# Long convolution on TensorE: 128-row products with four column blocks on shifted copies, in place of diagonal weights

## The chip, the cores and the metric

The kernel runs on one core of a Trainium2 chip. The metric is device time in microseconds of one execution. Five engines run side by side: TensorE (matrix products into PSUM), VectorE (DVE), ScalarE (ACT), GpSimd (POOL) and SyncE (SP), which here only issues transfers. They are ordered by semaphores alone.

## The reference

Two transformer-like blocks over 256 tokens with 1,024 features, all in float32. The part that the change touches is the convolution module at the very start:

```python
def conformer_conv(x, norm_g, pw1_w, pw1_b, dw_w, dw_b, ln_g, ln_b, pw2_w, pw2_b):
    a, b = jnp.split(rmsnorm(x, norm_g) @ pw1_w + pw1_b, 2, axis=-1)
    h = a * jax.nn.sigmoid(b)
    h = lax.conv_general_dilated(h, dw_w[:, None, :], window_strides=(1,),
        padding=[(CONV_WIDTH - 1, 0)], dimension_numbers=('NWC', 'WIO', 'NWC'),
        feature_group_count=h.shape[-1]) + dw_b
    h = jax.nn.silu(layernorm(h, ln_g, ln_b))
    return h @ pw2_w + pw2_b
```

The convolution is depthwise and causal with CONV_WIDTH = 31: each feature has its own 31 taps, output[t] = sum over j of tap[j] times input[t - 30 + j]. After it come two feed-forward layers, an attention with three branches, a gated recurrence, cross attention and a last feed-forward layer.

## The kernel before

Features lie on partitions: 1,024 features are KT = 8 feature tiles of 128, each with S = 256 tokens in the free dimension. `u` [128, 8, 30 + 256] holds the gated input of the convolution behind 30 zero columns, `v` [128, 8, 256] its output, `tapT` the taps, one column per tap.

**Weights and their queue.** Every dense weight comes in chunks of 1 MB, in one fixed order, through four `raw` buffers, all issued by SP (L464 to L472). Chunks 0 to 7 are `pw1` (one per feature tile, two transfers of 512 KB each), 8 to 11 `pw2` (one transfer each), from 12 on the first feed-forward layer. Chunk c waits until DVE has finished splitting chunk c - 4. ACT takes the high part of a chunk (`split_hi`, L568), DVE the low part (`split_lo`, L936), and TensorE forms three products (L1461 to L1463) for each pair of tiles. There are three split slots, so that ACT's split of a chunk also waits for TensorE to have finished the chunk three before. `through(c)` stands in the streams of ACT and DVE wherever the splits up to chunk c are to be done.

**The first stage.** TensorE runs eight `feature_pair("pw1", ft, ...)` of 48 products each. After each, ACT takes a sigmoid (L636, `gate_act`) and DVE multiplies (`glu_pw1`, L986, counted by `glu_done`) into `u`. `glu_pw1(ft)` first does the split of chunk ft + 2.

**The convolution.** Feature tiles 0 to 3 and 28 taps of tile 4 (`SHARED`) are done by DVE, one multiply-add of 128x256 per tap and tile (L1015, L1018), in two passes over the 31 taps: tiles 0 and 1, then 2, 3 and 4. Every fourth tap one entry of `tasks` is put in: the remaining `glu_pw1` and the splits of the `pw2` chunks. Tiles 5 to 7 and the last 3 taps of tile 4 are done by TensorE as products with a diagonal 128x128 matrix per tap (L1593, 96 products), after all eight `pw1`. ACT builds the diagonals (`diagonals`, L626) in the buffer `act`, eight to a group, between its splits, and copies the finished sums out (L661, `conv_out`).

**After it.** TensorE sums `v` over the features with a constant matrix (L1603; in order the tiles 5, 6, 7, 0 to 4), DVE subtracts the mean (L1038), ACT squares, and so on to `pw2`, which waits for all of it. Nothing of the layers behind can start earlier.

Of the kernel before, what the change touches and what calls it, by code (L numbers as in the profile page):

```python
# [33 lines left out]
P = 128  # L34
# [17 lines left out]
TAPG = 8  # L52
# [15 lines left out]
def build_kernel(nc, a, out):  # L68
# [8 lines left out]
    with ctx:  # L77
# [81 lines left out]
        CONV_DVE, SHARED, SHARED_TAPS = 4, 4, 28  # L159
        pe_taps = {ft: list(range(SHARED_TAPS if ft == SHARED else 0, TAPS)) for ft in range(CONV_DVE, KT)}  # L160

        groups = [(ft, js[i:i + TAPG]) for ft, js in pe_taps.items() for i in range(0, len(js), TAPG)]
        NDIAG = 7
        diag = actf[:, 0:NDIAG * TAPG * P].rearrange("p (g t c) -> p g t c", t=TAPG, c=P)

# [41 lines left out]
        conv_link = sem("conv_link")  # L207
        conv_dve = sem("conv_dve")
# [22 lines left out]
        diag_built = sem("diag_built")  # L231
        diag_used = sem("diag_used")
# [227 lines left out]
        def _(sp):  # L460
            for t in range(TT):
                sp.dma_start(h[:, t, :], a["x"][0].rearrange("(t p) n -> p t n", p=P)[:, t, :]
                             ).then_inc(x_loaded[t], 16)
            for c, parts in enumerate(chunks):  # L464
                if c >= RAWS:
                    last = c - RAWS
                    if is_split[last]:
                        sp.wait_ge(*lo_count(last))
                    else:
                        sp.wait_ge(*freed[last])  # L470
                for place, src in parts:
                    sp.dma_start(place(raw[c % RAWS]), src).then_inc(raw_loaded[c % RAWS], 16)  # L472
# [86 lines left out]
        def _(sc):  # L559
# [61 lines left out]
            def diagonals(g):  # L621
                ft, js = groups[g]
                if g >= NDIAG:
                    sc.wait_ge(diag_used, g - NDIAG + 1)
                for q, j in enumerate(js):
                    x = nc.scalar.activation(diag[:, g % NDIAG, q, :], ident[:, :], ACT.Copy,  # L626
                                             scale=tapT[:, ft, j:j + 1])
                x.then_inc(diag_built, 1)


            for ft in range(KT):
# [20 lines left out]

            built = NDIAG
            for ft in range(CONV_DVE, KT):
                used = max(g for g in range(len(groups)) if groups[g][0] == ft) + 1
                while built < min(used + NDIAG, len(groups)):
                    diagonals(built)
                    built += 1
                if ft != SHARED:
                    sc.wait_ge(diag_used, used)  # L660
                    nc.scalar.activation(v[:, ft, :], bank[ft][:, 0:S], ACT.Identity,  # L661
                                         bias=vecT[:, col["a_dw_b"] + ft:col["a_dw_b"] + ft + 1]
                                         ).then_inc(conv_out, 1)
# [261 lines left out]
        def _(ve):  # L925
# [47 lines left out]
            nc.vector.memset(u[:, :, 0:PAD], 0.0).then_inc(pads_zero, 1)  # L973

# [25 lines left out]
            tasks = [lambda ft=ft: glu_pw1(ft) for ft in range(2, KT)]  # L1000
# [3 lines left out]
            for fts in ((0, 1), (2, 3, SHARED)):  # L1004
                for j in range(TAPS):
                    if j % 4 == 3 and tasks:
                        tasks.pop(0)()
                    if SHARED in fts and j == SHARED_TAPS:
                        fts = fts[:-1]
                    for f, ft in enumerate(fts):  # L1010
                        tap, dst, src = tapT[:, ft, j:j + 1], v[:, ft, :], u[:, ft, j:j + S]
                        b = col["a_dw_b"] + ft
                        if j == 0:
                            ve.wait_ge(glu_done, ft + 1)
                            x = nc.vector.tensor_scalar(dst, src, tap, vecT[:, b:b + 1], ALU.mult, ALU.add)  # L1015
                        else:
                            ve.wait_ge(conv_link, tap_done[ft])
                            x = nc.vector.scalar_tensor_tensor(out=dst, in0=src, scalar=tap, in1=dst,  # L1018
                                                               op0=ALU.mult, op1=ALU.add)
                        if j == TAPS - 1:  # L1020
                            x.then_inc(conv_dve, 1)
                        else:
                            taps_done += 1
                            tap_done[ft] = taps_done
                            x.then_inc(conv_link, 1)

            ve.wait_ge(diag_used, 1 + max(g for g in range(len(groups)) if groups[g][0] == SHARED))
            ve.wait_ge(conv_link, tap_done[SHARED])
            nc.vector.tensor_tensor(v[:, SHARED, :], v[:, SHARED, :], bank[SHARED][:, 0:S],
                                    ALU.add).then_inc(conv_dve, 1)  # L1030
# [408 lines left out]
        def _(te):  # L1439
# [135 lines left out]

            for ft in range(KT):
# [378 lines left out]
```

## Time and profile before

| | us |
|---|---|
| median of 3 runs | 1180.0 (1174.27 to 1182.57) |
| the profiled execution, its own time | 1178.26 |
| its span, first to last instruction | 1176.5 |
| TensorE busy in the span | 1108.6 (94%) |
| DVE / ACT / POOL busy | 665.4 / 548.7 / 64.7 |
| mean granted TensorE clock | 0.973 |

The profile is one execution, recorded instruction by instruction. A float32 product is recorded as two instructions (two passes), so the 96 products of L1593 are x192. A name such as `v` or `act` is the tensor's, without its slice. "Idle before" is an engine's idle time ahead of an instruction, with what ended it. Times in rows are from the span's start.

### The profile page before, as it was taken

The page shows a single profiled execution, that of the slowest core. Times are in us where ns is not written, and L with a number is a line of the kernel's source. Part 1 is how long each engine was busy: PE and PEld are TensorE (multiplying, and loading weights), DVE is VectorE, ACT ScalarE, POOL GpSimd, SP SyncE. Part 2 cuts the span into 40 slices and gives each one's busy share as a digit, 9 for nine tenths or more (in the row PEclk, how much of TensorE's full clock was granted, in tenths as well). Part 3 has the DMA queues.
Part 4 walks back from the last instruction along what each step waited for, and adds up shares of the span by engine and source line. Part 5 has one row for each costly group of instructions (what it writes and reads, how often), then busy time and mean ns, then how long its engine had stood idle before and what let it go on. Part 6 is the DMA issues. An engine that isn't in the chain of part 4 may idle for free.

```text
span 1176.5 us, 17460 instructions
## 1 busy us (share of the span) xinstructions
PE 1108.6 (94%) x7303; PEld 989.8 (84%) x7303; DVE 665.4 (57%) x1104; ACT 548.7 (47%) x888; POOL 64.7 (5%) x102
## 2 busy tenths in 40 slices
PE   6997899999999977999999979999999999999997
PEld 6996589999989954789999979899667888999996
DVE  3999555445445489454555556646454454555554
ACT  5871354444443478354433445535344544444442
POOL 3000073000010000000000010000000000000000
PEclk9999899999999899799999999999899999999999
DMA  8740146566673600546666553654215424555640
GB/s 230 226 128 8 57 123 179 181 204 180 187 151 97 227 1 2 170 135 185 192 195 180 179 179 101 206 179 130 86 40 173 138 80 143 180 193 174 206 144 36
DMA packets 188313, 170.76 MB, mean 145 GB/s; under 512 B 15398, under 2 KB 164006, under 8 KB 188234
## 3 DMA queue, kind: packets, MB, share of 16 engines
q1 hardware_dynamic: 187128, 167.20, 46.4%
q10 hardware_dynamic: 1010, 2.43, 0.6%
q8 instruction: 58, 0.95, 0.3%
q14 instruction: 21, 0.17, 0.0%
q0 software_dynamic: 96, 0.02, 0.0%
HBM read 168.58 MB, written 1.05 MB: 144 GB/s over the span
## 4 chain that ended last, share of the span: by engine, by line
PE 79%; DVE 13%; ACT 3%; POOL 1%; issue 1%; POOLq 0%; ACTq 0%; DVEq 0%
PE bank L1461 24%; PE bank L1462 24%; PE bank L1463 24%; DVE v L1018 5%; DVE split_lo L936 2%; PE bank L1476 1%; ACT scaled L586 1%; DVE soft L1155 1%; DVE soft L1136 1%; PE bank L1639 1%; PE bank L1827 1%; POOL msq L501 1%; PE bank L1826 1%; POOL rstd L504 1%; DVE h L968 0%
## 5 line engine op out<-in xcount | busy, mean ns | idle before, releaser
L936 DVE TENSOR_TENSOR split_lo<-raw,split_hi 128x2048 fp32r<-128x2048 f32 (+1 forms) x157 | 356.1, 2270 | 240.4 <-ACT split_hi L568 240.3
L1461 PE MATMUL bank<-xn_hi,split_hi 128*128 128x256 f32 x1440 | 411.2, 286 | 3.2 <-DVE xn_lo L953 3.1
L1462 PE MATMUL bank<-xn_lo,split_hi 128*128 128x256 f32 x1440 | 408.6, 284 | 0.0
L1463 PE MATMUL bank<-xn_hi,split_lo 128*128 128x256 f32 x1440 | 408.5, 284 | 0.0
L568 ACT ACTIVATE split_hi<-raw 128x2048 fp32r<-128x2048 f32 (+1 forms) x157 | 296.4, 1890 | 148.6 <-PE bank L1463 142.2
L1461 PEld LDWEIGHTS bank<-xn_hi,split_hi 128*128 128x128 f32 x1440 | 277.4, 193 | 7.0 <-issue 5.3
L1462 PEld LDWEIGHTS bank<-xn_lo,split_hi 128*128 128x128 f32 x1440 | 277.5, 193 | 1.3
L1463 PEld LDWEIGHTS bank<-xn_hi,split_lo 128*128 128x128 f32 x1440 | 277.4, 193 | 0.0
L1461 PE MATMUL bank<-split_hi,ffa_hi 128*128 128x512 f32 x320 | 124.9, 390 | 0.0
L1462 PE MATMUL bank<-split_lo,ffa_hi 128*128 128x512 f32 x320 | 124.9, 390 | 0.0
L1463 PE MATMUL bank<-split_hi,ffa_lo 128*128 128x512 f32 x320 | 124.5, 389 | 0.0
L1461 PE MATMUL bank<-split_hi,xn_hi 128*128 128x512 f32 (+3 forms) x240 | 92.3, 385 | 5.1 <-DVE xn_lo L936 5.1
L1463 PE MATMUL bank<-split_hi,xn_lo 128*128 128x512 f32 (+3 forms) x240 | 90.5, 377 | 0.0
L1462 PE MATMUL bank<-split_lo,xn_hi 128*128 128x512 f32 (+3 forms) x240 | 90.5, 377 | 0.0
L684 ACT ACTIVATE soft<-bank 128x256 f32<-128x256 f32 x44 | 16.9, 385 | 137.1 <-PE bank L1463 137.1
L1463 PEld LDWEIGHTS bank<-split_hi,ffa_lo 128*128 128x128 f32 x320 | 60.1, 188 | 12.8
L1461 PEld LDWEIGHTS bank<-split_hi,ffa_hi 128*128 128x128 f32 x320 | 60.2, 188 | 11.6
L1462 PEld LDWEIGHTS bank<-split_lo,ffa_hi 128*128 128x128 f32 x320 | 60.2, 188 | 11.1
L1461 PEld LDWEIGHTS bank<-split_hi,xn_hi 128*128 128x128 f32 x240 | 47.6, 198 | 17.4 <-DVE xn_lo L936 5.0
L1018 DVE SCALAR_TENSOR_TENSOR v<-u,tapT,v 128x256 f32<-128x256 f32 x147 | 58.9, 474 | 0.0
L501 POOL TENSOR_SCALAR msq<-ssq 128x1 f32<-128x1 f32 x20 | 10.5, 527 | 811.2 <-ACT scaled L586 811.0
L1463 PEld LDWEIGHTS bank<-split_hi,xn_lo 128*128 128x128 f32 x240 | 47.5, 198 | 8.2
(257 smaller groups left out, 1042.5 us busy)
## 6 DMA issues: line engine op xcount, KB each, us to landing
raw<-in_ffn_w_in SPq DMA_DIRECT2D x88, 512.0 KB, 5.1
raw<-in_w_ff SPq DMA_DIRECT2D x32, 1024.0 KB, 5.2
raw<-in_ffn_w_out SPq DMA_DIRECT2D x22, 1024.0 KB, 4.9
raw<-in_w_in SPq DMA_DIRECT2D x14, 1024.0 KB, 5.2
raw<-in_a_pw_w SPq DMA_DIRECT2D x16, 512.0 KB, 6.9
raw<-in_w_xkv SPq DMA_DIRECT2D x8, 1024.0 KB, 5.3
raw<-in_a_pw_w SPq DMA_DIRECT2D x4, 1024.0 KB, 5.2
raw<-in_b_w_in SPq DMA_DIRECT2D x4, 1024.0 KB, 6.7
```

What stands on the lines that cost most here:

```text
L501: nc.gpsimd.tensor_scalar(msq[:, c:c + 1], ssq[:, c:c + 1], EPS, None, ALU.add).then_inc(ms_ready, 1)
L504: nc.gpsimd.tensor_tensor(rstd[:, c:c + 1], msq[:, c:c + 1], nhalf[:, 0:1], ALU.pow).then_inc(rstd_ready, 1)
L568: nc.scalar.activation(split_slot[m % SPLITS][0][:, 0:n], raw[c % RAWS][:, 0:n], ACT.Copy).then_inc(split_hi, 1)
L586: nc.scalar.activation(scaled[:, t, :], src[:, t, :], ACT.Square, scale=D ** -0.5, accum_out=ssq[:, TT * k + t:TT * k + t + 1]).then_inc(s ...
L684: nc.scalar.activation(softf[:, b], bank[ft % 4][:, 0:S], ACT.Silu).then_inc(gate_act, 1)
L936: return nc.vector.tensor_tensor(dst, src, hi.bitcast(F32), ALU.subtract)
L1018: x = nc.vector.scalar_tensor_tensor(out=dst, in0=src, scalar=tap, in1=dst, op0=ALU.mult, op1=ALU.add)
L1136: x = nc.vector.tensor_tensor_reduce(out=scores_of(i)[:, piece], in0=src, in1=bias, scale=-DH ** -0.5, scalar=3e38, op0=ALU.add, op1=ALU.m ...
L1155: x = nc.vector.tensor_scalar(scores_of(i)[:, piece], scores_of(i)[:, piece], coef[:, i % 2, n:n + 1], None, ALU.mult)
L1461: mm(dst, left[0], right[0], start=start, stop=False)
L1462: mm(dst, left[0], right[1], start=False, stop=False)
L1463: return mm(dst, left[1], right[0], start=False, stop=stop)
```

## The change

Tiles 0 and 1 stay on DVE, in one pass over the taps. Tiles 2 to 7 (`CONV_PE`) all go to TensorE in another form. For each such tile, SP copies `u` into `quad_u`: for each group of 32 channels q and each shift g of 0 to 3, partitions 32g to 32g+31 hold the 32 channels shifted by g columns, 16 transfers of 32 partitions and up to 1,136 bytes a row. With these, one product of 128 rows (4 shifts x 32 channels) and 32 columns covers four taps of 32 channels; eight such rounds cover the 31 taps (the weight of the 32nd is zero), and four blocks of 32 columns, one for each q, stand side by side in the array: 32 products for a tile. DVE builds the weights of a tile in one multiplication with broadcast operands (`quad_weights`, 128x1024), from `quad_taps`, which TensorE rearranges once (`turn_quads`, 16 products of 64 columns) and DVE copies out of PSUM. The buffers have three slots (`RING`).

The products `conv(0)` to `conv(2)` are put behind `pw1` of tiles 4, 5 and 6, `conv(3)` to `conv(5)` after the last `pw1`. On SP the copies for tile ft stand ahead of the load of chunk ft + 5 and wait for `glu_done` of that tile. ACT builds no diagonals any more and copies six tiles out instead of three.

```diff
-        CONV_DVE, SHARED, SHARED_TAPS = 4, 4, 28
+        QUAD, NQ = 32, P // 32
+        ROUNDS, SPAN = 8, S + 28
+        CONV_DVE = [0, 1]
+        CONV_PE = [2, 3, 4, 5, 6, 7]
+        RING = 3
...
+            def shift_copies(n):
+
+                ft, slot = CONV_PE[n], n % RING
+                sp.wait_ge(glu_done, ft + 1)
+                if n == 0:
+                    sp.wait_ge(quad_set, RING)
+                if n >= RING:
+                    sp.wait_ge(quad_done, n - RING + 1)
+                for g in range(NQ):
+                    w = SPAN - (g == NQ - 1)
+                    for q in range(NQ):
+                        sp.dma_start(quad_u[QUAD * g:QUAD * g + QUAD, slot, q, 0:w],
+                                     u[QUAD * q:QUAD * q + QUAD, ft, g:g + w]).then_inc(quad_loaded[slot], 16)
+
+            conv_at = {ft + RAWS + 1: n for n, ft in enumerate(CONV_PE)}
...
+                if c in conv_at:
+                    shift_copies(conv_at[c])
                 for place, src in parts:
                     sp.dma_start(place(raw[c % RAWS]), src).then_inc(raw_loaded[c % RAWS], 16)
...
-                if ft == 0:
-                    sc.wait_ge(pre_copied, 3)
-                if ft < NDIAG:
-                    diagonals(ft)
...
+            for n, ft in enumerate(CONV_PE):
+                sc.wait_ge(quad_done, n + 1)
+                nc.scalar.activation(v[:, ft, :], bank[4 + n % 4][:, 0:S], ACT.Identity,
+                                     bias=vecT[:, col["a_dw_b"] + ft:col["a_dw_b"] + ft + 1]
+                                     ).then_inc(conv_out, 1)
...
+            for g in range(NQ):
+                q = slice(QUAD * g, QUAD * g + QUAD)
+                x = nc.vector.tensor_copy(quad_one[q, :], ident[q, q])
+            link(x)
+            ve.wait_ge(quad_taps_turned, 1)
+            link(nc.vector.tensor_copy(quad_taps[:, :, :, :].rearrange("p a f j -> p (a f j)"),
+                                       bank[7][:, 0:NQ * KT * ROUNDS]))
+            link(nc.vector.memset(quad_taps[P - QUAD:P, :, :, ROUNDS - 1:ROUNDS], 0.0))
+
+            def quad_weights(n):
+
+                if n >= RING:
+                    ve.wait_ge(quad_done, n - RING + 1)
+                shape = [P, NQ, ROUNDS, QUAD]
+                nc.vector.tensor_tensor(quad_w[:, n % RING, :, :, :],
+                                        quad_taps[:, :, CONV_PE[n], :].unsqueeze(3).broadcast_to(shape),
+                                        quad_one[:, :].unsqueeze(1).unsqueeze(1).broadcast_to(shape),
+                                        ALU.mult).then_inc(quad_built, 1)
+
+            tasks = []
+            for ft in range(2, KT):
+                tasks.append(lambda ft=ft: glu_pw1(ft))
+                if ft - 2 < len(CONV_PE):
+                    tasks.append(lambda n=ft - 2: quad_weights(n))
             tasks += [lambda j=j: through(chunk_of["pw2"][j]) for j in range(3)]
...
-            for fts in ((0, 1), (2, 3, SHARED)):
+            for j in range(TAPS):
+                if j % 4 == 1:
+                    for task in tasks[:2]:
+                        task()
+                    tasks = tasks[2:]
+                for ft in CONV_DVE:
...
+            def conv(n):
+
+                slot = n % RING
+                te.wait_ge(quad_built, n + 1)
+                te.wait_ge(quad_loaded[slot], 16 * NQ * NQ * (n // RING + 1))
+                if n >= 4:
+                    te.wait_ge(conv_out, n - 3)
+                for j in range(ROUNDS):
+                    for q in range(NQ):
+                        x = mm(bank[4 + n % 4][QUAD * q:QUAD * q + QUAD, 0:S], quad_w[:, slot, q, j, :],
+                               quad_u[:, slot, q, 4 * j:4 * j + S], start=j == 0, stop=j == ROUNDS - 1)
+                x.then_inc(quad_done, 1)
+
             for ft in range(KT):
...
+                if ft == 1:
+                    turn_quads()
+                if 4 <= ft < KT - 1:
+                    conv(ft - 4)
+            for n in range(3, len(CONV_PE)):
+                conv(n)
...
-                for q, j in enumerate(js):
-                    x = mm(bank[ft][:, 0:S], diag[:, g % NDIAG, q, :], u[:, ft, j:j + S],
-                           start=j == pe_taps[ft][0], stop=j == TAPS - 1)
-                x.then_inc(diag_used, 1)
```

The sum over features (L1603 of before) takes the tiles 2 to 7 first and 0 and 1 last.

## Rows read from the trace of the kernel before

**Rows 1.** The page: busy time by engine, and the chain that ended last

```profile
PE 1108.6 (94%) x7303; PEld 989.8 (84%) x7303; DVE 665.4 (57%) x1104; ACT 548.7 (47%) x888; POOL 64.7 (5%) x102
PE 79%; DVE 13%; ACT 3%; POOL 1%; issue 1%; POOLq 0%; ACTq 0%; DVEq 0%
```

**Rows 2.** The chain that ended last, 30 to 125 us: start, length, what

```profile
33.78 0.74 DVE v L1015 x2
34.51 1.58 DVE v L1018 x4
36.09 2.20 DVE split_lo L936
38.69 3.16 DVE v L1018 x8
...
84.14 26.93 DVE v L1018 x68
111.11 1.92 PE bank L1603 x6
113.05 2.36 DVE v L1038 x2
```

**Rows 3.** Groups by line and shape, 0 to 160 us: busy, mean ns, idle before

```profile
L1018 DVE SCALAR_TENSOR_TENSOR v<-u,tapT,v 128x256 f32<-128x256 f32 x147 | 58.9, 474 | 0.0
L1593 PE MATMUL bank<-u,act 128*128 128x256 f32 x192 | 41.6, 378 | 0.0
L626 ACT ACTIVATE act<-ident,tapT 128x128 f32<-128x128 f32 x96 | 29.3, 389 | 5.1 <-PE bank L1593 2.6 <-DVE posT L997 1.4 <-issue 1.0
L1038 DVE TENSOR_TENSOR v<-v,bank 128x1024 f32<-128x1024 f32 x2 | 2.4, 1217 | 1.3 <-PE bank L1603 1.3
```

**Rows 4.** Timeline of ACT: sigmoids of pw1 tiles 2 and 7, last copy out

```profile
36.37 0.47 ACT L636 ACTIVATE soft<-bank,vecT 128x256 f32<-128x256 f32 x1 [0.90 <-PE bank L1463]
65.17 0.47 ACT L636 ACTIVATE soft<-bank,vecT 128x256 f32<-128x256 f32 x1 [1.14 <-PE bank L1463]
106.64 0.47 ACT L661 ACTIVATE v<-bank,vecT 128x256 f32<-128x256 f32 x1 [12.92 <-PE bank L1593]
```

**Rows 5.** Timeline of TensorE, 66 to 70 us: start, length, merged instructions

```profile
65.62 4.70 PE L1593 MATMUL bank<-u,act 128*128 128x256 f32 x21
```

**Rows 6.** Timeline, attention, 424 to 427 us: products of 64 columns, two destinations in turn

```profile
425.19 0.20 PEld L1711 LDWEIGHTS bank<-pt,v 128*64 128x64 f32 x4 [0.21 <-issue]
425.19 0.65 PE L1711 MATMUL bank<-pt,v 128*64 128x256 f32 x4
425.67 0.39 PE L1713 MATMUL bank<-pt,v 128*64 128x128 f32 x4
425.89 0.60 PE L1711 MATMUL bank<-pt,v 128*64 128x256 f32 x4
426.32 0.39 PE L1713 MATMUL bank<-pt,v 128*64 128x128 f32 x4
```

**Rows 7.** Timeline of SP: start, length until the queue took it, merged issues

```profile
8.05 0.78 SPq L477 DMA_DIRECT2D pt<-in_cmp_pos_k  x2
8.87 0.88 SPq L477 DMA_DIRECT2D pt<-in_cmp_pos_v  x2
61.38 0.99 SPq L472 DMA_DIRECT2D raw<-in_ffn_w_in  x2
379.75 2.22 SPq L472 DMA_DIRECT2D raw<-in_b_w_out  x1
```

**Rows 8.** Timeline of ACT's own queue: a transfer to 64 partitions

```profile
65.82 0.61 ACTq L646 DMA_DIRECT2D phi<-in_phi_v_w  x1
```

**Rows 9.** DMA issues, 0 to 170 us: KB each, median us from issue to landing

```profile
raw<-in_ffn_w_in SPq DMA_DIRECT2D x12, 512.0 KB, 4.8
raw<-in_a_pw_w SPq DMA_DIRECT2D x4, 1024.0 KB, 5.2
pt<-in_a_norm POOLq DMA_DIRECT2D x1, 4.0 KB, 5.9
```

**Rows 10.** Windows: us, busy of PE, PEld, DVE, ACT, POOL, granted clock, DMA share, GB/s

```profile
20.00:30.00 10.00, 10.00 (x86) 9.78 (x86) 5.46 (x5) 7.15 (x8) 0.00 (x0) 1.00 1.13 294
100.00:110.00 10.00, 8.76 (x41) 7.29 (x39) 10.00 (x26) 0.47 (x1) 0.00 (x0) 1.00 0.00 0
110.00:120.00 10.00, 3.38 (x9) 1.86 (x10) 6.63 (x11) 3.61 (x4) 0.00 (x0) 0.61 0.00 1
```

More of the change, by code:

```diff
@@ L51 @@
 SLOT = 2048
-TAPG = 8
 XSCALE = (D // XH) ** -0.5
@@ L156, in build_kernel @@
         pw2_row = qT[0:1, 0:4, :].rearrange("p a b -> p (a b)")
-        CONV_DVE, SHARED, SHARED_TAPS = 4, 4, 28
[L160 to L164, printed above, removed]
+        QUAD, NQ = 32, P // 32
[3 more added lines that the diff above has]
+        RING = 3
+        quad_u = actf[:, 0:RING * NQ * SPAN].rearrange("p (r a x) -> p r a x", a=NQ, x=SPAN)
+        at = RING * NQ * SPAN
+        quad_w = actf[:, at:at + RING * NQ * ROUNDS * QUAD].rearrange("p (r a j c) -> p r a j c", a=NQ, j=ROUNDS, c=QUAD)
+        quad_taps = ptf[:, 512:512 + NQ * KT * ROUNDS].rearrange("p (a f j) -> p a f j", a=NQ, f=KT)
+        quad_one = ptf[:, 768:768 + QUAD]
         window = ptf[:, 0:2 * 32 * 2 * NCMP].rearrange("p (b l g n) -> p b l g n", b=2, l=32, g=GROUPS)
@@ L207, in build_kernel @@
         conv_link = sem("conv_link")
+        quad_set = sem("quad_set")
+        quad_taps_turned = sem("quad_taps_turned")
+        quad_built = sem("quad_built")
+        quad_loaded = [sem(f"quad_loaded{i}") for i in range(RING)]
+        quad_done = sem("quad_done")
         conv_dve = sem("conv_dve")
@@ L230, in build_kernel @@
         glu_done = sem("glu_done")
-        diag_built = sem("diag_built")
-        diag_used = sem("diag_used")
         conv_out = sem("conv_out")
@@ L973, in _ @@
             nc.vector.memset(u[:, :, 0:PAD], 0.0).then_inc(pads_zero, 1)
+            for r in range(RING):
+                nc.vector.memset(quad_u[P - QUAD:P, r, :, SPAN - 1:SPAN], 0.0).then_inc(quad_set, 1)
             ve.wait_ge(pre_turned, 1)
@@ L1003, in _ @@
             taps_done, tap_done = 0, {}
-            for fts in ((0, 1), (2, 3, SHARED)):
[L1005 to L1030, printed above, removed]
+            for j in range(TAPS):
[4 more added lines that the diff above has]
+                for ft in CONV_DVE:
+                    tap, dst, src = tapT[:, ft, j:j + 1], v[:, ft, :], u[:, ft, j:j + S]
+                    b = col["a_dw_b"] + ft
+                    if j == 0:
+                        ve.wait_ge(glu_done, ft + 1)
+                        x = nc.vector.tensor_scalar(dst, src, tap, vecT[:, b:b + 1], ALU.mult, ALU.add)
+                    else:
+                        ve.wait_ge(conv_link, tap_done[ft])
+                        x = nc.vector.scalar_tensor_tensor(out=dst, in0=src, scalar=tap, in1=dst,
+                                                           op0=ALU.mult, op1=ALU.add)
+                    if j == TAPS - 1:
+                        x.then_inc(conv_dve, 1)
+                    else:
+                        taps_done += 1
+                        tap_done[ft] = taps_done
+                        x.then_inc(conv_link, 1)
@@ L1574, in turn_taps, with turn_quads @@
                 x.then_inc(pre_turned, 1)
+            def turn_quads():
+                te.wait_ge(pre_copied, 2)
+                for q in range(NQ):
+                    for g in range(NQ):
+                        x = mm(bank[7][QUAD * g:QUAD * g + QUAD, KT * ROUNDS * q:KT * ROUNDS * q + KT * ROUNDS],
+                               ident[:, QUAD * q:QUAD * q + QUAD], tapT[:, :, g:g + 4 * ROUNDS:4],
+                               start=True, stop=True)
+                x.then_inc(quad_taps_turned, 1)
+            def conv(n):
[5 more added lines that the diff above has]
+                for j in range(ROUNDS):
+                    for q in range(NQ):
+                        x = mm(bank[4 + n % 4][QUAD * q:QUAD * q + QUAD, 0:S], quad_w[:, slot, q, j, :],
+                               quad_u[:, slot, q, 4 * j:4 * j + S], start=j == 0, stop=j == ROUNDS - 1)
+                x.then_inc(quad_done, 1)
             for ft in range(KT):
```

31 lines of the change are left out of this document (4 added, 27 removed).

## The prediction

> **What bounds the kernel now.** I read the page first: TensorE is busy 94% of the span and holds 79% of the chain, DVE holds 13% of it [rows 1]. That is an average over stages. The chain in order of time shows this stage apart: from 33.78 us on it is DVE without a break, taps and splits, its last piece 68 taps in 26.93 us up to 111.11; TensorE then sums the features for 1.92 us and at 113.05 DVE subtracts the mean [rows 2]. So what the change is worth is how much earlier than 113.05 the mean can be subtracted. Behind it stands a chain that the change leaves alone. TensorE is not far behind DVE: its own 96 tap products take 41.6 us [rows 3] after the last `pw1`, whose sigmoid starts at 65.17, and their last copy out starts at 106.64 [rows 4]. Relieving DVE alone would give 4 us; both must become shorter. ACT's diagonals (29.3 us) lie beside them, and nothing waited for them at length [rows 3].
>
> **DVE, part by part.** A tap costs 0.395 us (8 in 3.16), a split 2.20 [rows 2]. It loses 152 - 62 = 90 taps, 35.6 us, and an addition of 0.4. It gains six `quad_weights`. The nearest row, 128x1024 with a broadcast operand, is 1.22 us [rows 3]; bounds 0.6 (if the operands could be read at double rate, which no row shows) and 1.22, I take 1.2: 7.2 us. The set-up (four 32x32 copies, a 128x256 copy out of PSUM, a memset, three waits on itself) I estimate at 1.2, from 0.4 for a 128x256 operation [rows 2]. Without waits DVE would end at 111.1 - 36.0 + 8.4 = 83.5. It does not run free, as `glu_pw1(7)` needs the last `pw1`.
>
> **TensorE.** A full product of 256 columns is two passes of (4.70 - 0.38)/20 = 0.216 us: 0.43 [rows 5, 3]. What four products of 32 columns cost is the question. No row has four; the nearest has two of 64 columns into the two halves of one bank [rows 6]: four passes of 256 columns take 425.89 to 426.32, 0.43 us, where one after another they would take 0.86. So different column blocks do run at once, and past the second pass of the one before. Four passes of 128 columns take 0.22, that is 0.055 per load and product, so issue would not hold a round of eight passes (0.44). Bounds of a round: 0.43 (all four at once) and 1.72 (one after another); I take 0.43, as the row shows full overlap. A tile is 8 x 0.43 = 3.5 us. The rule that speaks against it is in the Trainium skill, "TensorE: Matmul & The Clock Gate", Part 3: packing small matmuls; three column blocks there gained 2.38 times and four row blocks 3.07, not the full count. By 3.07 a tile would be 4.5 us and the end some 3 us later; the trace's two blocks gained 2.0 of 2.
>
> Each change of block form costs about 0.2 us (the load at 425.19 waited 0.21 with no releaser [rows 6]), two at each of the first three `conv`: 3.9 us each. `turn_quads`, four rounds of four products of 64 columns, is 4 x 0.11 plus two changes and its latency: 1.1.
>
> **SP, the new load.** 96 transfers more, each of 32 partitions, issued one by one ahead of weight loads. The nearest rows are the positions (32 partitions each): two in 0.82 us, then two in 0.93 [rows 7]. I take 0.46 in steady state; below lies 0.41, above 0.61 for one to 64 partitions [rows 8]. 16 of them: 7.4 us. A 1 MB chunk costs 1.0 to issue as two transfers [rows 7], about 0.4 as one. A transfer behind two that are not yet through can be held: 2.22 us in one row [rows 7]. The copies of tile 3 stand right behind chunk 7; I put 1.5 there. The source is SBUF, of which no row shows anything. Landing: a 512 KB load lands in 4.8 us, of which 1.8 is its bytes at 294 GB/s [rows 9, 10]; I take the remaining 3.0 for the last copy, with bounds 0.5 (about the issue alone) and 5.9 [rows 9]. The Trainium skill, "DMA: Bandwidth & Descriptors", anatomy of one DMA, puts the fixed cost of a transfer from POOL at about 2.0 us; by that the end would come 1 us earlier.
>
> **The schedule.** Sigmoids of `pw1` stood 5.76 apart, the third at 36.37 [rows 4]. With 1.1 for `turn_quads` they are at 37.5, 43.2 and 49.0 for tiles 2 to 4, then with `conv(0)` to `conv(2)` at 58.7, 68.3 and 78.0 for 5 to 7.
> - DVE: `glu_pw1(2)` ends two operations after 37.5, at 38.4. From there each period is a split, a product, a `quad_weights` and 8 taps, 2.2 + 0.4 + 1.2 + 3.2 = 7.0. It waits for tile 6 and tile 7 and has `glu_pw1(7)` at 78.9; then 1.2 + 3.2 + 3.2, the split of chunk 10 (2.2), four taps (1.6): 90.3.
> - SP: copies 38.4 to 45.8, chunk 7 and the hold to 48.3, copies to 55.7, chunk 8 (0.4), copies 56.1 to 63.5, then 71.3, 79.1 and the last 79.5 to 86.9. A cycle of 7.8 is just above the 7.0 of DVE, so SP falls behind and sets the end by itself; the copies of tile 7 could have started at 78.9.
> - Loads: chunk 7 is issued at 46 rather than at 34, chunk 8 at 56. They land by 53 and 61 and are wanted by DVE at about 57 and 64; chunk 9 is issued at 64, wanted at 73. No wait, with some 3 us in hand.
> - TensorE: `conv(3)` from 78, `conv(4)` to 86, then idle until the copies land at 89.9, `conv(5)` to 93.4. ACT's copy ends at 94.0. The last three tiles are summed as before, in 1.94 (111.11 to 113.05): 95.9.
>
> The gain is 113.05 - 95.9 = 17.1 us, taken from the profiled execution's own 1178.3 (span 1176.5 and 1.8 around it): 1161.2. The median of the runs is 1.7 higher and their spread is 8.3, so I leave **1161**. ACT loses 96 diagonals and gets three copies out: nothing, as it waits either way. The clock stands at full speed up to 110 and falls to a mean of 0.61 in 110 to 120, after TensorE had waited from about 107 to 111 [rows 10]. The wait here before `conv(5)` is about as long. If the clock has gone to 1.2 GHz by then, `conv(5)` costs 7 instead of 3.5: up to 3.5 later, kept in the range.
>
> **Rivals.**
> 1. SP's issue is dearer, or copies from SBUF hold each other up. For: 0.61 in rows 8, 2.22 in rows 7. Against: 0.46 for the same 32 partitions. The end moves by 96 times the difference; at 0.61 it is 14 us, leaving 3: 1175. If each copy took 0.65 nothing would be left.
> 2. Only two blocks run at once (two streams is all that any row shows). A tile is 6.9, 7.3 with changes: sigmoid 7 at 88, three more tiles to 109, copy and sum to 111.2: gain 2, 1176.
> 3. Slower: the blocks run one after another, because with 32 columns, or with four in turn, the two passes of a product hold the queue. A tile is 13.8, 14.2 with changes: sigmoid 7 at 109, then 41.4 to 150, the mean at 152.4: 39 us later, 1217. It decides from about 7.3 us per tile on. Against: rows 6, where the second destination did not wait for both passes of the first.
> 4. Faster: copies at 0.41 landing in 1 us. SP ends at 86.3 (its start at 79.7 set by `glu_pw1(7)` and chunk 11), sum at 93; DVE's 90.3 then stands 1 to 2 us behind: 1157.
>
> **How the numbers follow.** The forecast, 1161 with its own range 1154 to 1168 (0.5 to 3.5 from the clock, 2.5 either way from landing, 0.05 either way in issue is 4.8 us): 0.62. Rival 4: 0.08. Rival 1 (1168 to 1185): 0.11. Rival 2: 0.08. Rival 3: 0.06. Something else that the stages behind give back or lose: 0.05. A difference of about 1% (11.8 us) is what a measurement of this kernel can tell from none. Faster by more: 0.62 + 0.08 + 0.04 = 0.74. Within: most of rivals 1 and 2, 0.16. Slower: rival 3 and what is left, 0.10. The range, 1152 to 1175, takes in the forecast, rival 4 and half of rival 1 and leaves out just under 2 in 10.
>
> **What would show it.** The mean subtracted near 96. Passes of 128 rows and 32 columns: eight in 0.43 us right, in 0.86 or 1.72 rivals 2 or 3. SP's issues 0.46 apart, and TensorE idle before `conv(5)` for a transfer, not for DVE. DVE waiting once or twice for sigmoids, and its last tap near 90. No DVE or ACT wait for chunks 7 to 9; the hold behind chunk 7 about 1.5. The granted clock during `conv(5)`. The prediction is wrong if issue is above 0.5, if four blocks are not one, or if the late chunks make `pw1` wait.

## The result, and the profile after

The changed kernel takes 1184.56 us in the median of 12 runs (1181.76 to 1187.89), the kernel before 1176.98 (12 runs, 1174.27 to 1182.57). The ratio is 1.006, 95% interval 1.0042 to 1.0078: not 1.4% faster, as forecast, but slower by 0.6%, which is under the 1% that was taken as no change. The profiled execution took 1181.76 (span 1179.7, clock 0.967). It is the fastest of the 12, so that the two profiles differ by 3.5 us and the medians by 7.6.

Where the time is decided is the same place as before: DVE's subtraction of the mean. It was at 113.05 [rows 2] and is now at 117.70, 4.65 later; forecast was 95.9. The chain of the changed kernel in order of time, 80 to 121 us (start, length, what), shows what stands ahead of it:

```profile
by line: SPq L481 34.9%; PE bank L1618 27.3%; issue 15.9%; PE bank L1648 8.9%; DMA act<-u 5.9%; DVE v L1061 5.8%; ACT act L670 2.6%; SPq L495 1.4%; SPq L477 0.1%
...
94.28 0.59 SPq L481
94.87 0.04 issue
94.91 2.43 DMA act<-u
97.34 0.09 issue
97.44 5.84 PE bank L1618 x64
103.28 5.36 issue
108.64 5.37 PE bank L1618 x64
114.01 3.67 PE bank L1648 x16
117.70 2.36 DVE v L1061 x2
```

L481 is the copy in `shift_copies`, issued by SP; L1618 the products of `conv`; L1648 the sum over features. Before, this stretch was DVE without a break [rows 2]. Now it is a queue that issues transfers, one each 0.59 + 0.04 us, then one landing, then TensorE. SP's own timeline from 36 us on (start, length until the last of a group was issued, merged issues) tells the same for the whole stage:

```profile
38.35 10.12 SPq L481 DMA_DIRECT2D act<-u  x16
48.52 1.21 SPq L495 DMA_DIRECT2D raw<-in_a_pw_w  x2
49.83 10.97 SPq L481 DMA_DIRECT2D act<-u  x16
...
96.24 11.01 SPq L481 DMA_DIRECT2D act<-u  x16
```

SP is never idle between 38.35 and 107.25. 16 copies need at least 10.12 us, 0.633 each; with the chunk load behind them a cycle is 11.1 to 11.8, where TensorE's was to be 9.6 and SP's 7.8. The first start, 38.35, is where it was forecast (38.4). Everything behind queues up, the weight loads too. The waits, 0 to 130 us (engine and line, releaser: total us, times, longest):

```profile
ACT split_hi L591 <- DMA raw<-in_a_pw_w: 25.6, 6, 6.8
DVE v L1061 <- PE bank L1648: 20.1, 1, 20.1
PE bank L1618 <- DMA act<-u: 12.3, 4, 7.9
```

Two of ACT's six waits, 0.96 and 1.32 us, stand before 23 us, ahead of the first copy. The other four, 4.3 to 6.8 us each, are for the chunks behind the copies; the forecast had none of them. TensorE waits four times for copies by this view, and a fifth time ahead of `conv(5)`: those 5.36 us stand under "issue" in the chain above, and they end when the last copy has landed. The forecast had one such wait. DVE, which set the end before, has done its last tap at 97.6 and waits 20.1 us. Two sigmoids of `pw1` on ACT's timeline show when the delay began:

```profile
59.52 0.47 ACT L649 ACTIVATE soft<-bank,vecT 128x256 f32<-128x256 f32 x1 [2.49 <-PE bank L1486]
85.36 0.47 ACT L649 ACTIVATE soft<-bank,vecT 128x256 f32<-128x256 f32 x1 [4.79 <-PE bank L1486]
```

The one before them, of tile 4, is at 48.80 (forecast 49.0). For these two, tiles 5 and 7, the forecast was 58.7 and 78.0: late by 0.8 and by 7.4, so the delay grows with each cycle of SP. TensorE's timeline has the six convolutions; three of them:

```profile
85.85 3.66 PE L1618 MATMUL bank<-act 128*32 128x256 f32 x64 [0.53 <-DMA act<-u]
97.44 5.84 PE L1618 MATMUL bank<-act 128*32 128x256 f32 x64 [7.92 <-DMA act<-u]
108.64 5.37 PE L1618 MATMUL bank<-act 128*32 128x256 f32 x64 [5.36 <-issue]
```

64 passes of 256 columns take 3.66 us, and from the start of one round of eight passes to the next it is 0.43. All four blocks of 32 columns run at once, as the forecast took it. The last two are dearer by 2.2 and 1.7, and so is `conv(2)` (5.35 us from 74.03 on). The windows (us; busy of PE, PEld, DVE, ACT, POOL; granted clock, DMA share, GB/s) say why for `conv(4)`:

```profile
80.00:90.00 10.00, 8.99 (x109) 7.51 (x107) 6.42 (x10) 1.05 (x2) 0.00 (x0) 1.00 0.49 152
90.00:100.00 10.00, 2.56 (x25) 1.42 (x29) 7.60 (x15) 3.48 (x5) 0.00 (x0) 0.58 0.55 166
```

TensorE was busy for a quarter of 90 to 100 and its clock stood at a mean of 0.58, near the lower of its two levels (1.2 of 2.4 GHz). In 70 to 80, with `conv(2)`, the mean is 0.83, in 100 to 110, where `conv(5)` begins, 0.67. At the start of `conv(4)` a round of eight passes takes 0.85 us, at its end 0.43.

### The profile page after: what moved, and what is told of

It reads as the page before. It is cut to its first block, busy times and chain, and to the rows that moved or that the text cites. A ratio compares the mean times of both kernels' runs of the same rounds, so it can differ in the third digit from the quotient of the medians.

```text
span 1179.7 us, 17834 instructions
## 1 busy us (share of the span) xinstructions
PE 1095.2 (93%) x7527; PEld 970.5 (82%) x7527; DVE 638.2 (54%) x1028; ACT 521.9 (44%) x795; POOL 64.7 (5%) x102
## 4 chain that ended last, share of the span: by engine, by line
PE 81%; DVE 7%; SPq 5%; ACT 3%; issue 2%; POOL 1%; DMA 1%; POOLq 0%; ACTq 0%; DVEq 0%
PE bank L1484 24%; PE bank L1485 24%; PE bank L1486 24%; SPq L481 4%; PE bank L1499 2%; ACT scaled L609 1%; DVE soft L1178 1%; PE bank L1618 1%; DVE soft L1159 1%; PE bank L1684 1%; PE bank L1871 1%; PE bank L1872 1%; POOL msq L524 1%; POOL rstd L527 1%; DVE h L971 0%
## 5 line engine op out<-in xcount | busy, mean ns | idle before, releaser
L1485 PEld LDWEIGHTS bank<-split_lo,xn_hi 128*128 128x128 f32 x240 | 47.3, 197 | 7.3
```

Of the source, the lines that this page charges most:

```text
L1485: mm(dst, left[0], right[1], start=False, stop=False)
```

## The experiments

The theory after this result: the length of one issue on SP, 0.633 instead of 0.46, set the stage, whatever the transfers carry. Rivals were the bytes or rows of the copies, weight loads that come too late behind them, and TensorE's idle clock.

**1. Four transfers instead of 16.**

```diff
-                for g in range(NQ):
-                    w = SPAN - (g == NQ - 1)
-                    for q in range(NQ):
-                        sp.dma_start(quad_u[QUAD * g:QUAD * g + QUAD, slot, q, 0:w],
-                                     u[QUAD * q:QUAD * q + QUAD, ft, g:g + w]).then_inc(quad_loaded[slot], 16)
+                for q in range(NQ):
+                    sp.dma_start(quad_u[:, slot, q, :],
+                                 u[:, ft, min(q, 2):min(q, 2) + SPAN]).then_inc(quad_loaded[slot], 16)
```

> The changed kernel with 4 transfers of 128 partitions per tile instead of 16 of 32: the same bytes land, the same products run, but every row group holds the same shift, so the convolution of tiles 2 to 7 is not computed. Theory A (the number of issues on SP, 0.633 us each, sets the end of the stage): SP needs about 2.5 us per tile, the copies are always early enough, and TensorE and the sigmoids set the end: conv(5) from about 86 to 90, copy out 0.6, all eight feature sums behind it 3.7, the mean subtracted near 94 instead of 117.7, 1161 us. Rival B (the bytes of the copies or their landing beside the weight loads are what is slow): the bytes are unchanged, so the mean is subtracted no more than 3 us earlier than 117.7. Rival C (TensorE at 1.2 GHz in three of the six conv steps): only the last is on the chain, at most 2 us of the 24.

This kernel leaves out the shift between the groups of 32 rows, so that the convolution of tiles 2 to 7 is not computed and only the time counts. (The semaphore that `conv` waits for is counted to match.) Measured: 1158.97 us (4 runs), ratio to the kernel before 0.9832 (0.9796 to 0.9867). The mean is subtracted at 92.28. The same bytes and rows in 4 issues of 0.62 us (SP's timeline):

```profile
38.13 2.49 SPq L479 DMA_DIRECT2D act<-u  x4
...
78.25 2.48 SPq L479 DMA_DIRECT2D act<-u  x4
```

The count of issues makes the difference; the bytes and rows do not. The sigmoids are then as forecast, the last at 77.20 (forecast 78.0).

**2. What one issue costs.** In the kernel before, at about 85 us, transfers of eight forms, three of each, each three waited for.

```diff
+                if c == 14:
+                    forms = [("a", 32, 284, "u"), ("b", 32, 284, "x"), ("c", 32, 64, "u"), ("d", 32, 64, "x"),
+                             ("e", 64, 284, "u"), ("f", 128, 284, "u"), ("g", 31, 284, "u"), ("h", 32, 284, "o")]
```

> The kernel before with transfers added on SP where it idles (after chunk 14, from 85 us), three of each form and a wait for each form's landing: from u in SBUF 32 partitions x 1136 B, from DRAM 32 x 1136 B, from u 32 x 256 B, from DRAM 32 x 256 B, from u 64, 128 and 31 partitions x 1136 B, and from u to DRAM 32 x 1136 B. Which property makes the copy cost 0.633 instead of the 0.46 that was forecast from a DRAM source with 256 B? Theory A1 (both sides in SBUF): only the forms from u to SBUF show 0.63, the DRAM ones 0.46. A2 (the row length): both 1136 B forms show 0.63, both 256 B forms 0.46. A3 (partitions): 31 partitions near 0.30, 128 above 0.7. No change of the time, as DVE sets the stage.

Measured: 1180.04 us (one run), mean subtracted at 113.61, 0.56 later than in the kernel before. SP's timeline, each row three issues of one form (`u` is in SBUF, `in_x` and `bounce` in DRAM). In order: 32 partitions x 1,136 B from SBUF, the same from DRAM; 32 x 256 B from SBUF, the same from DRAM; 64, 128 and 31 partitions x 1,136 B from SBUF; 32 x 1,136 B from SBUF to DRAM:

```profile
84.91 2.30 SPq L489 DMA_DIRECT2D qT<-u  x3
90.51 1.26 SPq L489 DMA_DIRECT2D qT<-in_x  x3
93.24 1.79 SPq L489 DMA_DIRECT2D qT<-u  x3
96.23 1.97 SPq L489 DMA_DIRECT2D qT<-in_x  x3
99.56 1.80 SPq L489 DMA_DIRECT2D qT<-u  x3
102.84 1.77 SPq L489 DMA_DIRECT2D qT<-u  x3
106.17 1.93 SPq L489 DMA_DIRECT2D qT<-u  x3
113.13 1.25 SPq L489 DMA_DIRECT2D bounce<-u  x3
```

With both ends in SBUF three issues take 1.77 to 1.93 (the first row holds one of 1.04), with one end in DRAM 1.25 or 1.26 (the fourth row holds one of 1.14). Behind the first of a group, which is shorter, that is 0.63 and 0.46 from start to start. Neither 256 against 1,136 bytes a row nor 32 against 128 partitions changes it. These are three issues of each form; the 96 of the changed kernel have the same 0.63 in the median. So 0.46, read from rows 7, was right for what those rows showed, loads from DRAM, and wrong for a copy inside SBUF.

**3. Loads ahead of the copies.**

```diff
-                if c in conv_at:
-                    shift_copies(conv_at[c])
                 for place, src in parts:
...
+                if c in conv_at:
+                    shift_copies(conv_at[c])
```

> The changed kernel with one thing moved: at each chunk the weight load stands ahead of the copies and not behind them. The number of issues is the same. Theory A: the last copy is issued at about the same time plus the load of chunk 12 (1.2 us), mean subtracted 117.7 to 119.5, within 2 us of the changed kernel. Rival D (late weights: ACT waits 25.6 us for chunks 7 to 10 and hands this on to DVE and pw1): chunk 7 lands 10 us earlier and the others 10 us earlier, the waits of ACT for loads shrink below 5 us, and the mean comes 5 to 10 us earlier.

Measured: 1185.16 (10 runs), ratio 1.0058 (1.0033 to 1.0084), mean subtracted at 117.08, 0.6 sooner than 117.70. ACT's waits for weights are gone from this stage and almost nothing is won: the copies go out as before, 10.12 to 11.48 us for 16, and the delay sits in ACT's waits for `pw1` instead (the line of the waits: 24.1 in the changed kernel, 42.8 here).

```profile
ACT soft L649 <- PE bank L1486: 42.8, 7, 11.3
```

The late weights were a wait that hid another, not the cause.

**4. Copies by way of DRAM.** One write of the tile and four reads, all on SP.

```diff
+                sp.dma_start(bounce[ft], u[:, ft, :]).then_inc(bounced, 16)
+                sp.wait_ge(bounced, 16 * (n + 1))
...
-                    for q in range(NQ):
-                        sp.dma_start(quad_u[QUAD * g:QUAD * g + QUAD, slot, q, 0:w],
-                                     u[QUAD * q:QUAD * q + QUAD, ft, g:g + w]).then_inc(quad_loaded[slot], 16)
+                    sp.dma_start(quad_u[QUAD * g:QUAD * g + QUAD, slot, :, 0:w],
+                                 bounce[ft].rearrange("(q c) x -> c q x", q=NQ)[:, :, g:g + w]
+                                 ).then_inc(quad_loaded[slot], 16)
```

> The changed kernel, complete, with the copies made through DRAM: one write of the tile's 128 partitions, a wait for it, then 4 reads (one per shift) of 32 partitions x 4 blocks, 5 issues per tile instead of 16. Theory A: per tile 0.6 + about 2.5 for the landing + 4 x 0.6 = 5.5 us on SP, less than the 7 us period of DVE; the last copies land near 87, the mean is subtracted near 95, about 1162 us. Rival B (bytes): two times the bytes, so later than 117.7, above 1184.

Measured: 1167.91 (5 runs), ratio 0.9917 (0.9885 to 0.9949), mean subtracted at 105.43. SP's timeline shows the last tile's write and its reads:

```profile
81.30 0.44 SPq L480 DMA_DIRECT2D bounce<-u  x1
91.23 1.74 SPq L484 DMA_DIRECT2D act<-bounce  x4
```

Five issues cost 2.2 us in place of 10.1. But from the start of the write to the first read passed 1.9 us for the first tile, while no chunk load was under way, and 4.0 to 9.9 for the others, whose write stood behind a chunk load that had not landed. The expectation had 2.5 here, so its 95 for the mean was missed by 10; its rival, later than 117.7, is refuted too.

**5. Two queues, SP and ScalarE, eight copies each.**

```diff
-                    for q in range(NQ):
+                    for q in range(NQ // 2):
                         sp.dma_start(quad_u[...
...
+                if ft in CONV_PE:
+                    n = CONV_PE.index(ft)
+                    slot = n % RING
+                    sc.wait_ge(glu_done, ft + 1)
...
+                        for q in range(NQ // 2, NQ):
+                            sc.dma_start(quad_u[QUAD * g:QUAD * g + QUAD, slot, q, 0:w],
+                                         u[QUAD * q:QUAD * q + QUAD, ft, g:g + w]).then_inc(quad_loaded[slot], 16)
```

> The changed kernel, complete, with the 16 copies of a tile shared: SP issues the 8 of the blocks q = 0 and 1, ACT the 8 of q = 2 and 3, right after the tile's sigmoid. Theory A (what costs is the sequencer of one queue, 0.63 us per issue): the two queues issue side by side, 5.1 us per tile each, the copies of tile 7 are out near 84.5 and land near 87, the mean is subtracted between 94 and 98, 1160 to 1165 us. ACT's split of chunk ft + 3 comes 5 us later and can cost DVE up to 3 us per tile in the first tiles. Rival A' (the 0.63 us is spent in something that both queues share, such as the transfer engines): each issue takes about 1.2 us, the last copy goes out no earlier than 105, and the time stays near 1184.

Measured: 1177.52 (10 runs), ratio 0.9996 (0.9974 to 1.0018), mean subtracted at 111.55. That misses the 94 to 98 of the theory, and the time stays above its range. The two queues do issue side by side, each at a median of 0.645 from start to start (the row below holds two longer issues, 1.58 and 0.88). The rival is refuted. What holds the stage is now ACT, whose split of the chunk three ahead stands behind its eight issues (ACT's timeline, then its line of the waits):

```profile
47.71 6.29 ACTq L663 DMA_DIRECT2D act<-u  x8
54.10 1.92 ACT L591 ACTIVATE split_hi<-raw 128x2048 fp32r<-128x2048 f32 x1 [8.79 <-issue]
```

```profile
ACT split_hi L591 <- issue: 40.6, 5, 8.8
```

**6. The same with the split first.** The only difference from experiment 5:

```diff
                 if ft in CONV_PE:
+                    if ft < KT - 1:
+                        through(chunk_of["pw1"][ft] + 3)
                     n = CONV_PE.index(ft)
```

> Two queues again (SP issues 8 of a tile's 16 copies, ScalarE's queue the other 8), but the split of the chunk three ahead stands in ScalarE's order before its 8 copies and not behind them. Theory (in the run with two queues the issue cost was halved, and what then held the stage was that the split stood behind 8 issues of 0.63 to 0.65 us on ScalarE): the split comes in time, a tile's period falls to at most 9.6 us, the seventh sigmoid starts at 77 to 80, the last copies are out by 87, the mean is subtracted at 92 to 97, time 1159 to 1164. Rival (ScalarE is simply full with its own work and 8 issues, wherever the split stands): period still 10 to 11 us, mean subtracted near 111, 1175 to 1180.

Measured: 1166.66 (5 runs), ratio 0.9905 (0.9874 to 0.9936), mean subtracted at 99.87. The split was the bound: the period falls to 9.54 us (sigmoids at 58.47, 68.01, 77.55). The forecast of 92 to 97 was missed by 3, since at the end ACT's issues (eight copies until 83.6, then seven other transfers until 86.9) stand ahead of its copies out, for which `conv(4)` waits (TensorE's timeline, `conv(4)` and `conv(5)` in one row):

```profile
87.54 8.64 PE L1633 MATMUL bank<-act 128*32 128x256 f32 x128 [6.44 <-ACT v L679]
```

**7. Two queues, SP and GpSimd.** GpSimd has nothing to do in this stage.

```diff
+            for n, ft in enumerate(CONV_PE):
+                slot = n % RING
+                pool.wait_ge(glu_done, ft + 1)
...
+                    for q in range(NQ // 2, NQ):
+                        pool.dma_start(quad_u[QUAD * g:QUAD * g + QUAD, slot, q, 0:w],
+                                       u[QUAD * q:QUAD * q + QUAD, ft, g:g + w]).then_inc(quad_pool[slot], 16)
```

> SP issues 8 of a tile's 16 copies and GpSimd's queue, whose engine is idle in this stage, the other 8; ScalarE issues none. Theory (the bound is the sequencer time of each issue, 0.63 us on SP, and any second queue with about such a price halves it): SP's 8 take 5.1 us, ScalarE's splits come in time, last copies out by 87, mean subtracted at 92 to 97, time 1159 to 1164. Rival (a copy issued by GpSimd is dearer, over 1.2 us each, or lands late): 8 of them take 10 us or more, nothing is gained over the changed kernel, mean subtracted at 112 to 120, 1177 to 1187.

Measured: 1159.00 (4 runs, 1158.36 to 1163.35), ratio 0.985 (0.9814 to 0.9887), mean subtracted at 95.40. The rival is refuted. The instructions on the tile `act`, 30 to 100 us (count: duration in ns, least, median, most; first and last start), have both queues beside each other:

```profile
L482 SPq DMA_DIRECT2D act<-u x48: 507/592/1689, 38.4 to 82.9; - x48
L569 POOL DMA_DIRECT2D act<-u x48: 496/496/631, 38.6 to 82.1; - x48
```

GpSimd's issue is shorter than SP's, 0.496 against 0.592, and steadier. TensorE stays at full clock (1.00 in 80 to 90 and in 90 to 100), and waits only for its data:

```profile
88.05 3.66 PE L1633 MATMUL bank<-act 128*32 128x256 f32 x64 [2.66 <-DMA act<-u]
```

This version is faster than both kernels, than the kernel before by 1.5%.

**8. GpSimd alone,** all 16 copies of a tile there.

```diff
-                if c in conv_at:
-                    shift_copies(conv_at[c])
...
-                    for q in range(NQ // 2, NQ):
+                    for q in range(NQ):
```

> All 16 copies of a tile are issued by GpSimd's queue and none by SP, which keeps the chunk loads. The convolution is computed as in the changed kernel. With 8 of them GpSimd issued one every 0.49 us. Theory (the changed kernel is bound by how long one queue takes for its 16 issues): 16 x 0.49 = 7.8 us per tile, under TensorE's 9.5, so the period stays 9.5, the seventh sigmoid is at 77.5, the last copies are out at 78.7 + 7.8 = 86.5, landed near 91, sums over at 98.4, mean subtracted 98 to 99, time 1160 to 1164. Rival (GpSimd's queue slows down beyond 8 issues, because the transfers themselves cannot follow at that pace): 0.6 us or more apart, 10 us per tile, mean subtracted near 112 or later, 1177 or more.

Measured: 1166.19 (4 runs), ratio 0.9911 (0.9888 to 0.9933), mean subtracted at 99.86. The issue is as the theory says and does not slow down (GpSimd's timeline):

```profile
37.97 23.57 POOL L567 DMA_DIRECT2D act<-u  x48 [22.98 <-DVE u L1003]
63.97 7.81 POOL L567 DMA_DIRECT2D act<-u  x16 [2.44 <-DVE u L1003]
```

The mean comes 1 to 2 us later than expected and the time is 2 above. One event delays the rest (TensorE's timeline):

```profile
51.69 1.08 PE L1630 MATMUL bank<-act 128*32 128x256 f32 x8 [3.53 <-DMA act<-u]
```

The first 16 copies were out at 45.8 and the first convolution began at 51.69, 5.9 later, and then ran at a lowered clock (0.66 in 50 to 55): 5.02 instead of 3.66 us. Chunk loads were under way beside them. The landings in the traces fit that these delay the copies, on either queue. In the changed kernel, copies of SP's queue, issued in 38 to 48 us with no chunk load under way and in 49.8 to 53 with one (the last number is the median us from the start of the issue to the landing):

```profile
act<-u SPq DMA_DIRECT2D x12, 35.5 KB, 1.9
act<-u SPq DMA_DIRECT2D x5, 35.5 KB, 3.7
```

In this run, copies of GpSimd's queue, issued in 38 to 46 us with chunk loads under way and in 63.9 to 69 with none:

```profile
act<-u POOLq DMA_DIRECT2D x13, 35.5 KB, 4.3
act<-u POOLq DMA_DIRECT2D x11, 35.5 KB, 1.7
```

No run changes the loads alone. From the first convolution on everything stands 4.3 later than expected: the sigmoid of tile 7 at 81.77, the last copies out at 90.9. They landed within 1.7, which gave some of it back.

**9. Sums ahead of the last convolution,** in experiment 5 and in experiment 7. Of the 16 products of L1648, the 8 of tiles 2 to 5 go ahead of `conv(5)`.

```diff
             for n in range(3, len(CONV_PE)):
+                if n == len(CONV_PE) - 1:
...
+                    means(CONV_PE[:-2])
                 conv(n)
...
+            means(CONV_PE[-2:] + CONV_DVE).then_inc(stat_done, 1)
```

> As the run with two queues, and the feature sums of tiles 2 to 5 stand ahead of conv(5) instead of behind it. In the changed kernel all eight sums (16 passes, 3.67 us) stand behind conv(5); the forecast had put only three there. Expected: 4 sums, 1.7 us, leave the chain, unless DVE's last tap then ends later than conv(5): 1 to 2 us faster than the run with two queues.

> Two queues, SP and GpSimd, with 8 copies each, and the sums over the features of tiles 2 to 5 (8 of the 16 products) ahead of the last convolution, where TensorE waits 2.66 us for the last copies. Theory (at this point the sums stand on the path and the wait is free): mean subtracted 8 x 0.23 = 1.8 us sooner than 95.40, at 93.6, time 1156 to 1158, ratio to the kernel before about 0.983. Rival (as with SP and ScalarE as the two queues, where the same move gave nothing): mean subtracted at 95 to 96, 1158.5 to 1161.

Measured with SP and ScalarE: 1179.21 (10 runs), ratio 1.0017 (0.9996 to 1.0038), mean subtracted at 112.48, 0.9 later than without the move; missed. There the last copies had landed at 96.7, while `conv(4)` ran from 99.08 to 104.77 and experiment 5 had `conv(5)` right behind it: there was no wait to fill. With SP and GpSimd: 1158.28 (6 runs), ratio 0.9855 (0.9829 to 0.988), mean subtracted at 93.81, 1.6 sooner than experiment 7's 95.40, as expected:

```profile
85.06 1.99 PE L1652 MATMUL bank<-v,mean_w 128*128 128x256 f32 x8
87.97 3.66 PE L1633 MATMUL bank<-act 128*32 128x256 f32 x64 [0.91 <-DMA act<-u]
91.56 2.22 PE L1652 MATMUL bank<-v,mean_w 128*128 128x256 f32 x8
```

In the times the versions of experiment 7 and this one can't be told apart: the intervals of their ratios, both about 0.985, cover each other.

**10. DRAM copies on ACT's queue,** with the sums moved and SP left to the weights.

```diff
+                    sc.dma_start(bounce[ft], u[:, ft, :]).then_inc(bounced, 16)
+                    sc.wait_ge(bounced, 16 * (n + 1))
```

> The changed kernel, complete, with the copies made through DRAM (one write of 128 partitions, four reads), all on ACT's queue, SP issuing weight loads alone, and with the sums of tiles 2 to 5 ahead of conv(5). In the run with the DRAM copies on SP they stood in the ring behind 1 MB loads and took 4 to 10 us to land (write issued at 81.3, first read at 91.2). Theory A2 (that was the place in SP's ring): on the other ring a write lands in about 2.5 us and the reads in another 2.5, the last copies are there by 86, and the mean is subtracted at 91 to 94, 1157 to 1160 us. Rival (the write to DRAM itself is slow, or the loads hold it in the transfer engines whatever the ring): as slow as with SP, 105, 1168 us.

Measured: 1189.4 (5 runs), ratio 1.009 (1.0055 to 1.0124), mean subtracted at 120.54. Missed. ACT's timeline:

```profile
38.33 0.37 ACTq L641 DMA_DIRECT2D bounce<-u  x1
44.00 1.78 ACTq L649 DMA_DIRECT2D act<-bounce  x4
45.88 1.91 ACT L576 ACTIVATE split_hi<-raw 128x2048 fp32r<-128x2048 f32 x1 [8.10 <-issue]
```

5.7 us pass from the write to the first read, 4.4 to 5.7 for the other five tiles, though no load stands in this queue. But SP's queue had a weight load under way beside each of the six writes, and each time one landed within 0.6 us of the first read. So the theory, that the place in SP's queue was what made the write slow, fails, and of its rival the part that the loads hold the write whatever the queue fits. An engine that computes stands still for that time, and its split comes late.

**11. The clock.** The changed kernel with 16 products ahead of `conv(4)` and of `conv(5)` whose results nobody reads.

```diff
+                if n >= 4:
+                    te.wait_ge(glu_done, 6)
+                    for _ in range(16):
+                        mm(bank[1][:, 0:S], ident[:, :], u[:, 0, 0:S], start=True, stop=True)
```

> The changed kernel with 16 products of 256 columns that nobody reads put ahead of conv(4) and of conv(5), 6.9 us each, which fits into the waits of 7.9 and 5.4 us there. They leave everything else as it is. In the changed kernel conv(5) takes 5.37 us at a clock that has fallen, conv(0) 3.66 at full clock. Theory: with TensorE busy the clock stays at 2.4 GHz, conv(5) takes 3.66 and the sums behind it 3.4, so the mean is subtracted 1.7 to 2 us earlier than 117.7, near 116; the rest of the 24 us is untouched. Rival: the clock does not matter for this, no difference; or the added work runs past the landing and costs up to 1.5 us.

Measured: 1180.2 (10 runs), ratio 1.0042 (1.0015 to 1.0068), mean subtracted at 116.25, 1.45 sooner than 117.70. Both convolutions run at full speed:

```profile
98.20 3.66 PE L1622 MATMUL bank<-act 128*32 128x256 f32 x64 [1.46 <-issue]
101.80 7.17 PE L1615 MATMUL bank<-u,ident 128*128 128x256 f32 x32
108.90 3.66 PE L1622 MATMUL bank<-act 128*32 128x256 f32 x64
```

The first changes nothing at the end, as the last copies, still issued until 107 us, hold back `conv(5)`; only the second counts. The lowered clock is a consequence of the wait, worth 1.5 us at the mean, not its cause.

## Why the prediction was wrong, point by point

- **What bounds the kernel: right.** The subtraction of the mean is where the stage is decided. Behind it the profiled execution of before takes 1063.45 us (1176.5 - 113.05), that of after 1062.0. The medians differ by 3 us more than the 4.65 at the mean; what these 3 are I have not settled. The mean granted clock over a whole execution is 0.963 to 0.967 in the 12 runs of the changed kernel and 0.967 to 0.977 in those of the kernel before. In the two profiled executions that difference is this stage's own: ahead of the mean the clock is 1.00 before and 0.91 after, behind it 0.97 in both.
- **DVE: right.** `quad_weights` takes 1.21 us (forecast 1.2). In experiment 7, where it does not wait for late chunks, its last tap ends at 89.7 (forecast 90.3).
- **TensorE's products: right.** A round of eight passes takes 0.43. In experiment 7 a period with a convolution is 9.54 us (forecast 9.6 to 9.7). Rivals 2 and 3 did not happen.
- **SP's issue: the step that failed.** "I take 0.46 in steady state", with 0.61 above. The measured 0.633 was outside both bounds, and "issue is above 0.5" was one of the signs named for being wrong. The text itself said "the source is SBUF, of which no row shows anything", and yet took the value of the row with the same number of partitions. Partitions turned out to be what does not matter; the end that was unlike the row, the source, was. Of the 20.4 us by which the last copies went out later than forecast (107.3 against 86.9), 96 x (0.633 - 0.46) = 16.6 are this term. The rest are six single issues of 0.81 to 1.65 us among the short ones (3.9 in all above 0.59, where 1.5 was forecast for a hold) and the chunk loads between the copies (4.3 where 2.6 was forecast); rounding in the forecast takes 0.3 off. From there to the mean: landing 1.6 cheaper, `conv(5)` 1.9 dearer, what follows it 1.2 dearer. But for rounding, that is the 21.8 from 95.9 to 117.70.
- **The price at which nothing is left: near.** Rival 1 said the end moves by 96 times the difference and that nothing is left at 0.65; at 0.633 that would have left 0.5. There 4.65 were lost, 5.2 more, by the other terms just named. Its mechanism is what happened, with a chance of 0.11, too low for a term of 96 equal parts that no row showed.
- **The late chunks: wrong as a consequence.** "No wait, with some 3 us in hand" held for a cycle of 7.8, not of 11.1 to 11.8. Experiment 3 shows that the waits cost next to nothing of their own (0.6).
- **The last stretch.** Landing was put at 3.0 from the end of the last issue: in the changed kernel TensorE started 1.9 after it at `conv(4)` and 1.4 after it at `conv(5)`, in experiment 7 4.5. The sums were put at 1.94 "as before", but all eight tiles now stand behind `conv(5)` (L1648 x16, 3.67), 1.7 us that the diff showed. The clock took 1.7 at `conv(5)`, within the 3.5 that the range kept.
- With the copies on two queues the forecast for the stage comes true to half a microsecond, 95.40 against 95.9, partly by luck: copies out at 83.5, 3.4 sooner than forecast, landing 1.5 dearer, and `conv(5)` with what follows it 1.4 dearer. The time is then 1159.0, forecast 1161.

## What to carry to other kernels

Before many small transfers are put on a queue, multiply their number by the issue time of the same pair of source and destination, and ask which engine's queue is idle there. Up to the 145 KB tried here, the bytes did not change the issue time; the count made the sum. When a term of the sum is repeated 96 times and no row shows it, its being wrong deserves a large chance, not 0.11. And look at what is under way when a transfer must land: beside a chunk load it took longer on every queue here. A queue that belongs to an engine with its own work (ACT here) gives its time only if the work that others wait for is put ahead of the issues.

## What the runs showed of the hardware that I had not expected

- An issue on SP costs 0.59 + 0.04 us when both ends are in SBUF, 0.42 + 0.04 when one is in DRAM, the same for 256 and 1,136 bytes a row and for 32 to 128 partitions. On ACT's queue it is 0.645 from start to start in the median, on GpSimd's 0.487. SP's own median is 0.633 alone, 0.634 beside GpSimd's queue and 0.645 beside ACT's.
- Four blocks of 32 columns, each product of 128 rows in float32, run fully side by side: 64 passes of 256 columns in 3.66 us. At the 0.216 us of a full pass [rows 5, 3], one after another would be 13.8 and in pairs 6.9.
- A write of 146 KB to DRAM was usable 1.9 us after its issue with no weight load under way (one case, experiment 4), 4.0 to 9.9 behind a load in the same queue (five cases) and 4.4 to 5.7 with a load under way in another queue (six cases, experiment 10).
- TensorE could start 1.4 to 1.9 us after the last of SP's copies in the changed kernel, but 5.9 after GpSimd's first 16 in experiment 8 and 5.4 after GpSimd's last (4.5 after SP's) in experiment 7. The queue by itself does not account for it: with no chunk load under way a copy lands 1.9 us after the start of its issue on SP's queue and 1.7 on GpSimd's, with one 3.7 and 4.3 (experiment 8). What delayed the last copies of experiment 7, where the chunk load ahead of them had landed at 80.8, is open.
